# Row products for the second norm's shift and scale in a hybrid decoder layer, and a second bank for its gated-attention scores

## The reference, cut to what matters

```python
mod = (silu(c) @ ada_w + ada_b)                    # 1024 x 6144
sh_a, sc_a, gt_a, sh_f, sc_f, gt_f = split(mod, 6)
h = rmsnorm(x, norm_mix_g) * (1.0 + sc_a) + sh_a
proj = h @ w_in                                     # five chunks of columns
mix = concat(gla_mixer(...), swa_sink_mixer(...)) @ w_out
x = x + gt_a * mix
h = rmsnorm(x, norm_ffn_g) * (1.0 + sc_f) + sh_f
y = hier_moe(h, ...)                                # 32 experts, two of them for each token
x = x + gt_f * y
return rmsnorm(x, final_norm_g)
```

## Time and profile before

| what | us |
|---|---|
| time, median of 3 runs | 588.17 |
| lowest and highest run | 583.42, 588.43 |
| span of the profiled execution | 591.2 |
| TensorE busy in it (products) | 512.2 |
| VectorE busy | 284.6 |
| ScalarE busy | 147.1 |
| GpSimd busy | 80.2 |

### The profile page before, as it was taken

The page is one execution under the profiler, slowest core; times in us unless marked ns, Lnnn a source line. Parts: engine busy times, 40 slices in busy tenths (PEclk is TensorE's granted clock), DMA queues, the critical chain, the costliest instruction groups (busy, mean ns, idle before and its releaser), DMA issues.

```text
span 591.2 us, 7201 instructions
## 1 busy us (share of the span) xinstructions
PE 512.2 (87%) x2644; PEld 292.3 (49%) x2644; DVE 284.6 (48%) x700; ACT 147.1 (25%) x370; POOL 80.2 (14%) x128
## 2 busy tenths in 40 slices
PE   0497999999999998999983999999888987797981
PEld 0353585545656565455653555555444544344430
DVE  4589817484747473555554256323112321123275
ACT  2502214142434270222030312222111321120221
POOL 5000000000100000001122222222122221111101
PEclk9989889979999999999995899999889998798996
DMA  8999962950970005691017999999999999999673
GB/s 292 377 346 277 343 250 81 386 178 0 267 302 2 1 1 213 257 369 60 25 71 253 357 395 398 414 414 407 399 414 417 387 415 418 391 388 420 257 303 142
DMA packets 57981, 163.88 MB, mean 277 GB/s; under 512 B 10339, under 2 KB 13940, under 8 KB 51034
## 3 DMA queue, kind: packets, MB, share of 16 engines
q1 hardware_dynamic: 46632, 147.95, 66.0%
q0 software_dynamic: 6192, 12.38, 5.6%
q10 hardware_dynamic: 5122, 3.08, 1.8%
HBM read 155.48 MB, written 16.58 MB: 291 GB/s over the span
## 4 chain that ended last, share of the span: by engine, by line
PE 63%; DMA 14%; SPq 13%; DVE 3%; issue 3%; ACT 1%; ACTq 1%; POOL 1%; POOLq 0%; DVEq 0%
PE ps L1572 22%; PE ps L1840 10%; PE ps L1751 9%; DMA early<-in_w_up 6%; SPq L498 5%; PE ps L1853 4%; SPq L502 3%; DMA wide<-in_w_up 2%; SPq L504 2%; DMA xres<-in_x 2%; DMA wide<-y_rows 2%; PE ps L1829 2%; ACTq L772 1%; PE ps L1777 1%; PE ps L1617 1%
## 5 line engine op out<-in xcount | busy, mean ns | idle before, releaser
L1572 PE MATMUL ps<-ring,hreg 128*128 128x512 f32 (+1 forms) x320 | 136.6, 584 | 2.1 <-DVE hreg L1053 2.1
L1572 PEld LDWEIGHTS ps<-ring,hreg 128*128 128x128 f32 x320 | 63.5, 203 | 65.5 <-issue 60.0
L1440 DVE TENSOR_TENSOR turned<-turned,ps 64x256 f32<-64x256 f32 x33 | 14.0, 423 | 135.5 <-ACT turned L949 135.5
L1840 PE MATMUL ps<-ring,proj 128*64 128x256 f32 x288 | 70.6, 401 | 7.8 <-DMA ring<-in_w_up 7.2
L1841 PE MATMUL ps<-ring,proj 128*64 128x256 f32 x288 | 70.6, 401 | 0.0
L1840 PEld LDWEIGHTS ps<-ring,proj 128*64 128x64 f32 x288 | 40.2, 144 | 31.0 <-DMA ring<-in_w_up 7.6
L1024 DVE SCALAR_TENSOR_TENSOR wide<-wide,csil 128x512 f32<-128x512 f32 x72 | 49.1, 746 | 2.5 <-DMA wide<-in_ada_w 2.5
L949 ACT ACTIVATE turned<-ps 64x256 f32<-64x256 f32 x33 | 12.4, 375 | 143.7 <-PE ps L1841 143.7
L701 POOL DMA_INDIRECT y_rows<-proj,hreg x31 | 30.9, 997 | 109.8 <-DVE proj L1446 109.8
L643 POOL TENSOR_TENSOR rstd<-ssq,halfm 128x1 f32<-128x1 f32 (+1 forms) x13 | 10.0, 766 | 232.6 <-DVE ssq L1323 140.5
L1841 PEld LDWEIGHTS ps<-ring,proj 128*64 128x64 f32 x288 | 40.3, 145 | 0.0
(11 more groups left out here) (331 smaller groups left out, 792.7 us busy)
## 6 DMA issues: line engine op xcount, KB each, us to landing
wide<-in_ada_w SPq DMA_DIRECT2D x24, 1024.0 KB, 8.7
ring<-in_w_gate SPq DMA_DIRECT2D x17, 1024.0 KB
ring<-in_w_up SPq DMA_DIRECT2D x17, 1024.0 KB
ring<-in_w_down SPq DMA_DIRECT2D x17, 1024.0 KB, 23.5
wide<-in_w_down SPq DMA_DIRECT2D x10, 1024.0 KB
ring<-in_w_in SPq DMA_DIRECT2D x4, 2048.0 KB, 9.6
proj<-in_w_gate SPq DMA_DIRECT2D x5, 1024.0 KB
proj<-in_w_up SPq DMA_DIRECT2D x5, 1024.0 KB
```

Source lines behind the costliest of these rows:

```text
L1572: mm = pe.matmul(ps[bank_of(st)][:, 0:CW[ch]], hT[:, k, b * P:(b + 1) * P], win_sb[ch][:, k, :], start=k == 0, stop=k == KD - 1)
L1840: pe.matmul(ps[bank][0:TILE, 0:F], hx[k], w_cols(w, 0, k), start=k == 0, stop=k == KD - 1)
```

## The change

Pieces 6 to 9 get a row product each, as the others have, and ScalarE copies each bank to half of `mo_t` (128 by 1024, all 1024 sums in every partition). GpSimd multiplies that by the identity, spread over groups of eight columns, so that partition p keeps only its own eight values, and adds halves to each other, 512 columns, then 256, down to 8, into `fcol`: eight operations in a chain, each waiting for the one before. ScalarE's copies of pieces 8 and 9 wait until the first chain is done, since both use `mo_t`. `amp` moves to just ahead of `bias_sum`. The two banks of projections and mods now have 28 turns in place of 26.

The odd heads' scores go to bank 5. TensorE's wait between even and odd goes; the next block's `attn_score`, which also writes bank 5, waits for both masked copies, and VectorE's one masked copy of 512 columns becomes two of 256.

```diff
-     ("proj", 1, 2), ("mod", 7), ("proj", 1, 3), ("rope",), ("decay_logit",), ("amp",), ("log_sigmoid",)] +
+     ("proj", 1, 2), ("mod", 6), ("mod", 7), ("proj", 1, 3), ("rope",), ("decay_logit",), ("log_sigmoid",)] +
...
-     ("proj", 2, 2), ("mod", 9), ("attn_score", 0), ("attn_exp", 0), ("ada_sum", 10), ("ada_sum", 11),
+     ("proj", 2, 2), ("mod", 8), ("mod", 9), ("attn_score", 0), ("attn_exp", 0), ("ada_sum", 10), ("ada_sum", 11),
...
-    [("bias_sum",), ("out_proj", 0, 0, 8), ("bias",), ("mix_turn", 1), ("out_proj", 0, 1, 8), ("gate_scale", 2),
+    [("amp",), ("bias_sum",), ("out_proj", 0, 0, 8), ("bias",), ("mix_turn", 1), ("out_proj", 0, 1, 8), ("gate_scale", 2),
...
+FOLDS = 8
...
         # GpSimd
+                elif st in (("mod", 7), ("mod", 9)):
+                    part_n = PARTS[st[1] // 2]
+                    pool.wait_ge(turn_free, TURN[st] + 1)
+                    by_col = mo_t.rearrange("p (q k) -> p q k", k=KD)
+                    pool.tensor_tensor(by_col, by_col, ident[:, :].unsqueeze(2).broadcast_to([P, P, KD]), ALU.mult)\
+                        .then_inc(fcol_ready, 1)
+                    steps = FOLDS * (4 - part_n)
+                    for i, w in enumerate(64 * KD >> a for a in range(FOLDS - 1)):
+                        pool.wait_ge(fcol_ready, steps + i + 1)
+                        to = mo_t[:, 0:w] if w > KD else fcol[:, 4 - part_n, :]
+                        pool.tensor_tensor(to, mo_t[:, 0:w], mo_t[:, w:2 * w], ALU.add).then_inc(fcol_ready, 1)
...
         # ScalarE, copies of mods
-                            act.activation(fcol[:, 4 - PARTS[i // 2], :], bank[:, 0:KD], ACT.Copy)\
-                                .then_inc(turn_free, 1)
+                            if PARTS[i // 2] == 3:
+                                act.wait_ge(fcol_ready, FOLDS)
+                            act.activation(mo_t[:, half], bank[:, :], ACT.Copy).then_inc(turn_free, 1)
...
         # VectorE: piece, amp, bias_sum, masked copies
-                    last = i - 2 if PARTS[(i - 2) // 2] not in (3, 4) else (i - 2) // 2 * 2 + 1
-                    dve.wait_ge(turn_ready, TURN[("mod", last)] + 1)
+                    dve.wait_ge(turn_ready, TURN[("mod", i - 2)] + 1)
...
-                    dve.wait_ge(turn_free, TURN[("mod", 7)] + 1)
+                    dve.wait_ge(fcol_ready, FOLDS)
...
-                    dve.wait_ge(turn_free, TURN[("mod", 9)] + 1)
+                    dve.wait_ge(fcol_ready, 2 * FOLDS)
...
-                    dve.copy_predicated(out=aT, mask=causal[:, :].bitcast(U32).unsqueeze(1).broadcast_to([P, GH, P]),
-                                        data=ps[2][:, :].rearrange("p (h t) -> p h t", h=GH)).then_inc(gla_masked, 1)
+                    for odd in range(2):
+                        src = ps[5 if odd else 2][:, :].rearrange("p (i o t) -> p o i t", i=2, o=2)[:, odd]
+                        dve.copy_predicated(out=aT.rearrange("p (i o) t -> p o i t", o=2)[:, odd],
+                                            mask=causal[:, :].bitcast(U32).unsqueeze(1).broadcast_to([P, 2, P]),
+                                            data=src).then_inc(gla_masked, 1)
...
         # TensorE: mod, attn_score, gla_scores, gla_output
-                    if PARTS[i // 2] in (3, 4):
-                        pe.wait_ge(acc_ready, i + 1)
-                        for k in range(KD):
-                            mm = pe.matmul(bank[:, k:k + 1],
-                                           acc.rearrange("p a n -> p (a n)").rearrange("p (q k) -> p k q", k=KD)[:, k, :],
-                                           ones[:, 0:1], start=True, stop=True)
-                    else:
-                        pe.wait_ge(acc_ready, i + 1)
-                        mm = pe.matmul(bank[:, :], ones[:, :], acc[:, i % 2, :], start=True, stop=True)
-                    mm.then_inc(turn_ready, 1)
+                    pe.wait_ge(acc_ready, i + 1)
+                    pe.matmul(bank[:, :], ones[:, :], acc[:, i % 2, :], start=True, stop=True).then_inc(turn_ready, 1)
...
+                        pe.wait_ge(gla_masked, 2 * n)
...
-                            mm = pe.matmul(ps[2][:, h * P:(h + 1) * P], gkT[rows, h // 2, :], gqT[rows, h, :],
+                            mm = pe.matmul(ps[5 if odd else 2][:, h * P:(h + 1) * P], gkT[rows, h // 2, :], gqT[rows, h, :],
                                            start=True, stop=True)
                         mm.then_inc(gla_scored, 1)
-                        if odd == 0:
-                            pe.wait_ge(gla_scored, 2 * n + 1)
...
-                    pe.wait_ge(gla_masked, n + 1)
+                    pe.wait_ge(gla_masked, 2 * (n + 1))
```

More of the change, by code:

```diff
@@ L315, in layer_kernel @@
             sem(n) for n in ('e_down', 'e_out'))
-        ov_free = sem('ov_free')
+        ov_free, fcol_ready = (
+            sem(n) for n in ('ov_free', 'fcol_ready'))
         fg_in, y_in0, y_in1, y_in2 = (
```

## The result

The changed kernel takes 580.58 us, median of 4 runs (579.84 to 580.96), against 588.3 for the kernel before (583.42 to 588.69): ratio 0.9889, interval 0.9841 to 0.9938. In a later comparison with more runs it was 582.12 us (12 runs) against 586.36 (21), ratio 0.9937 (0.9904 to 0.9969). So it is faster, by 4 to 8 us between the medians, and these two numbers already tell that something varies. The ratios are those on record with their 95% intervals, and not the plain quotient of the two medians beside them (0.987 in the first case). One run of the kernel before (592.42 us) and one of the experiment with the scores alone (589.13 us) lie over 1.5% above the fastest run of their kernel, and all ratios and counts here leave them out. The forecast was 580.2.

A forecast was written before the change was run, and what follows sets the result against it. TensorE was taken to bound the changed stretch, 74 to 139 us, without a hole. 5.15 + 1.85 + 1.5 + 0.96 = 9.5, less 1.5 for folds: 8.0 us off 588.17, 580.2 us; own range 578.7 to 582.2, with run spread 575.5 to 587.0.

The forecast's parts named there:

- First batch: Sums 6 and 7: one-column products, projection and line 1633, 12.25 us, become 7.10 with row products; gain 5.15 us.
- the granted clock says why: Projections behind one-column batches are slow because the clock falls to 1.2 GHz: 6.75 us against a warm 3.66.
- Second batch: Sums 8 and 9: 3.57 us of one-column products become 1.72 us of row products; gain 1.85 us.
- Behind it: Scores to sum 10: warm clock gains 1.5 us, VectorE being last; GpSimd's folds delay sum 10 by 1.5 (0 to 3.5).
- Scores: Four score rounds in two banks: TensorE's own wait goes, about 0.24 us each, 0.96 us; the masked copies stay hidden.
- Carried on unchanged: Expert stage: its weight stream at 408 GB/s starts earlier by the whole gain, 8.0 us.
- rival C: Expert weights: the gain stops there if something that doesn't move sets the DMA stream; 587.5 us, chance 0.07.
- less than 6 us earlier: Sign of a wrong forecast, at the first expert product: it comes less than 6 us earlier.
- Rival B: Sum 10: VectorE bounds the second batch in full, clock falls again; gain 2.9 to 4.7, 584.4 us, chance 0.2.
- a clock near 0.5: Sign of a wrong forecast: granted clock near 0.5 behind any row product, where 1.00 was expected behind the new ones.
- D: Copy of sum 8: GpSimd's folds hold ScalarE and the kernel is slower, 598 us; chance 0.05.
- E: Columns not the low clock's cause; it falls again behind row products, at line 1662; gain 3.4, 584.8 us, chance 0.08.

The follow-up runs named there:

- the experiment with the scores alone: The kernel before with only the odd heads' second score bank added, one-column products kept: 585.14 us, ratio 0.9941 (584.02 without the 589.13 us run).
- the second profile of before: The kernel before, with no edit, profiled once more: 585.43 us, span 583.7.
- the second profiles of before and after: Unedited repeats: the kernel before at 585.43 us, and the changed kernel, profiled again in the comparison with median 582.12 us (12 runs).

## Why the prediction was right, and which steps were not

The total came out (580.2 against 580.58), but that is in part luck. Two terms of the sum were far off, in opposite directions, and the gain of 8.0 us, a ratio of 0.9864, is met by the first runs alone (4 against 4): with more runs it is 4.2 us, and 0.9864 lies outside that interval (0.9904 to 0.9969).

- **First batch, 5.15 us: right against the earlier trace rows, wrong as a cost of the kernel.** From the batch to the end of the decay logits it is 12.25 us there and 7.40 now, a gain of 4.85; the decay logits took 1.92 us again, where I had 1.72. But in the second profile of before the same three steps take 9.28 us. Without falls the term is 1.9 us. The step that failed is "the granted clock says why": the level was read rightly and columns as its cause fit the runs, but I took one execution for all, although the times ran from 583.42 to 588.43.
- **Second batch, 1.85 us: right.** 3.57 became 1.81.
- **Behind it, 1.5 us less 1.5 for the folds: right in mechanism.** VectorE is last at sum 10. I took 9.75 us from the scores; without folds it is 9.49. The folds' 1.5 measured 1.8. The 1.5 of clock gain again depends on the execution: the second profile of before takes 9.48 us from the scores to sum 10, with nothing to gain.
- **Scores, 0.96 us: mis-sized by three.** I took away the 0.25 us of the earlier trace rows that is labelled as a wait. What goes is 0.75 a round: without the wait the loads and products of the two halves run side by side, in pairs 0.01 us apart. The cover was as predicted: the copies cost nothing.
- **Sum.** In executions without a fall in this stretch: 1.9 + 1.8 - 1.8 + 3.0 = 4.9 us; the table of equal clocks says 3.2 to 4.4. The second profiles of before and after, each with a fall near 230 us and one near 310 us, have 239.41 us (319.90 - 80.49) and 234.44 (318.53 - 84.09) from the first batch to the first expert product, 4.97 less. What the medians show beyond that goes with the clock.
- **Carried on unchanged: right.** From the first expert product to the end of the span it is 263.6 us now (579.1 - 315.46) and 265.5 before, and 264.0 and 263.8 in the second profiles: rival C fell. But that product comes 10.24 us earlier between the first profiles and 1.37 (319.90 to 318.53) between the second ones, where the changed kernel alone had a fall near 60 us: the sign "less than 6 us earlier" cannot be read from one pair.
- **Rival B** took place in part: the folds cost 1.8 us and not 3.5, but behind the stand of 3.15 us the clock fell in three of five executions, at 1.7 us (8.56 in place of 6.87). So one sign of being wrong came, a clock near 0.5 (0.53) behind a row product, that of sum 10. B's gain of 2.9 to 4.7 us is also nearer the 4.2 of the larger comparison than the forecast's 8.0. **D:** a chain of GpSimd takes 6.0 us alone and 7.7 and 7.1 beside VectorE, and ScalarE waited for none. **E:** directly behind the new row products the clock fell in none of eight executions, but behind columns it fell in one of three only, so half of its reasoning holds.

The Trainium skill, "SBUF — State Buffer", section "Who interferes with whom", says that VectorE and GpSimd exclude one another for whole instructions when they meet on the shared port, and that issue order decides who waits. On the first the traces agree: the rotary product of 2.96 us for 0.49 ends at 90.34, behind the multiplication's end at 89.98. On the order they do not decide, since that product's record starts at 87.38, ahead of the multiplication's at 87.92, while the operation of 1.24 us starts at 114.39, behind an addition that starts at 114.34. The contention brought sum 10 toward the middle of my bounds, not to the upper one.

What stays open: why one execution falls behind the columns and the next, with the same 3.58 us, doesn't, and how much of the difference between the medians the columns' falls make. Other falls, in the first projections near 60 us and at the stand late in the mixer, came and went between executions in the same manner, and no run was made to separate them.

## What to carry to other kernels

A low clock in one profile is a cost only if a second profile of the same kernel has it too; where the times of one kernel lie 5 us apart, profile twice, or compare runs at equal mean clock. A wait of an engine on itself can cost more than its idle time in the trace (here 0.75 us a round for 0.25), since it also stops the overlap of loads and products across it. When GpSimd gets work, place it beside VectorE's slack and not beside the sum that TensorE waits for, and look for the DMA that is late next.

## What the runs showed that was not expected

- Half-height weight loads of the two halves run side by side: eight in 0.53 us where four took 0.52.
- GpSimd's chain alone: 1.97 us for the multiplication of 1024 columns (1.9 ns a column), 3.64 for six halving additions, 0.20 for the last.
- A small operation can pay for contention out of proportion: 1.24 us for eight columns beside a chain, against 0.17 or 0.18 elsewhere.
- The mean clock of a whole run tells a good part of its time: between the lowest and the highest of the three classes of the kernel before lie 5.7 us in the medians.
